# A three-block model on one core: convolution taps beside the in-projection, modulation rows beside the second down projection, running sums for norms

## The chip, the core and the metric

The kernel runs on one core of a Trainium2 chip. The metric is device microseconds of one execution; three runs gave 4223.4, 4220.96 and 4223.6 us, median 4223.4. All data is fp32; large products are made from a rounded part and a rest of each operand (three matmuls for one).

## The reference, cut to what matters

A sequence of 512 tokens of width 1024 goes through three blocks. What the change touches:

```
# first block
x = layer_norm(ALPHA*x + 0.5*swiglu(x, ffn1...), ln1)
q, f_raw, i_val, g_out, conv_val, conv_gate = split(x @ w_in)      # 6 x 512 columns
o_a = hgrn2(q, f_raw, i_val) ... * sigmoid(g_out)
u = conv_val * sigmoid(conv_gate)
c = depthwise_causal_conv(u, conv_w)  + conv_b                     # 31 taps, 512 channels
o_b = silu(layer_norm(c))
x = layer_norm(ALPHA*x + concat(o_a, o_b) @ w_out, ln2)
x = layer_norm(ALPHA*x + 0.5*swiglu(x, ffn2...), ln3)
# second block
mod = silu(c) @ w_ada + b_ada                                      # 1024 x 6144, one row of c
h = rms_norm(x) * (1 + scale1) + shift1 ; x = x + gate1 * (mixer(h) @ w_out)
h = rms_norm(x) * (1 + scale2) + shift2 ; x = x + gate2 * experts(h)
# third block
x = x + mixer3(rms_norm(x)) @ w_out ; x = x + relu(rms_norm(x) @ w_ff1)**2 @ w_ff2
out = rms_norm(x)
```

## The kernel before

Features lie on the 128 partitions, tokens along the free axis, so x is 8 feature blocks of 128 x 512.

`linear` (L274) is one projection. Weights come as units through a ring of four slots, fetched by SyncE: 8 feature blocks (512 KB) a unit, or 11 (704 KB) in the down projections of the first block, where an output block is two units (m = 2). VectorE splits each unit into a rounded part (L382) and a rest (L71), two units at a time being held; TensorE does 24 or 33 matmuls of 128 x 512 with it (L347); ScalarE (`act_out`) or VectorE (`dve_out`) evicts. VectorE's order in a body is: split the next block's units, wait for this block's matmuls, evict. Bodies are run in hardware loops. Stages given as `stages` run ahead of the first unit in the same block of code: VectorE splits the first two units, and then does its part of the stages.

`Norm` (L102) sums over features on TensorE with a matrix of ones: with centering first the mean (L152, 8 matmuls) and the subtraction (L194), then squares on ScalarE (L171), their sum (L158, 8 matmuls), root (L175), reciprocal on VectorE (L198), scaling (L205), bias (L180), and the split into parts (L184, L71). In the profile one fp32 matmul is two records, so 8 are "x16".

In the first block, `in_projection_and_modulation` (L497) runs the 24 units of the in-projection; beside each, SyncE fetches two rows of w_ada (128 x 1024, 512 KB each, ring of four) and VectorE multiplies and adds them (L530, L532). `hgrn_and_conv` (L607) then runs four blocks of code, each ending in a barrier:
- a first step: 48 one-column matmuls that end the modulation (L636), gates, logarithm, scan (L650), u (L654);
- transposes of v and k into rows (L717, copies L695, exponential L706);
- the score loop, 7 levels and a first one: VectorE makes distances (L760, L761), ScalarE the exponential (L807), GpSimd one product (L747) and VectorE the other (L794), TensorE the scores (L834), VectorE the masked copies (L766). Beside it run the convolution's taps: 62 on VectorE for feature blocks 2 and 3 (L776, L780), 62 on TensorE for 0 and 1 (L839), each with a diagonal matrix from ScalarE (L811), two in turn;
- the output step (L861 to L923).

After it comes the convolution's norm in a block of its own, then the out-projection, whose weights are fetched when it begins. The second feed-forward follows with its down projection (8 blocks of 66 matmuls, VectorE evicting at L433), then the second block, whose first stage is the third layer norm followed by an RMS norm.

What orders the work is the order written for each engine and semaphore waits between them:

```
for k in (2 * j, 2 * j + 1):                          # L526 and on, beside unit j of body i
    dve.wait_ge(ada_landed[k % 4], i * 32 + (k // 4 * 16 + 16))
    ...
    dve.wait_ge(multiplied, i * DB + (k + 1))
    dve.sem_inc(rows_used, 1)
```

Of the kernel before, what the change touches and what calls it, by code (L numbers as in the profile page):

```python
# [76 lines left out]

class Split:
# [17 lines left out]
    def vector(self, dve):  # L96
        for k in range(self.kb):
            dve.wait_ge(self.hi_ready, k + 1)
            self.parts.rest(self.p.nc, (slice(None), k, slice(None)), self.src[:, k, :]).then_inc(self.lo_ready, 1)


class Norm:  # L102
# [7 lines left out]
    def __init__(self, p, ctx, src, dst, kb, width, eps, gain, bias=None, center=True, func=ACT.Identity,  # L110
                 parts=None, first=0, after=None, squares=None, rstd=None, root_in_bank=False):
        self.p, self.src, self.kb, self.width, self.eps = p, src, kb, width, eps
        self.gain, self.bias, self.center, self.func = gain, bias, center, func
        self.parts, self.first, self.after = parts, first, after
        halves = 1 if width <= 512 else 2
# [8 lines left out]
        else:  # L124
            self.rstd = p.sb(ctx, "rstd", [P, width])[:] if rstd is None else rstd
        self.mean_ready, self.centered, self.sq_ready, self.sq_used, self.eps_set, self.rms_ready, self.rstd_ready, \
            self.scaled, self.done, self.hi_ready, self.lo_ready = p.sems(
                ctx, "mean_ready", "centered", "sq_ready", "sq_used", "eps_set", "rms_ready", "rstd_ready",
                "scaled", "done", "hi_ready", "lo_ready")
# [16 lines left out]
    def tensor(self, pe):  # L146
        nc, kb = self.p.nc, self.kb
        if self.center:
# [5 lines left out]
            last.then_inc(self.mean_ready, 1)  # L154
        for k in range(kb):
# [6 lines left out]
    def scalar(self, act):  # L162
        nc, kb, center = self.p.nc, self.kb, self.center
        for k in range(kb):
# [9 lines left out]
        act.wait_ge(self.sq_used, kb)  # L174
# [12 lines left out]
    def vector(self, dve):  # L187
# [3 lines left out]
        if self.center:  # L191
            dve.wait_ge(self.mean_ready, 1)
            for k in range(kb):
                nc.vector.scalar_tensor_tensor(out=self.halved(self.dst[:, k, :]), in0=self.total(0), scalar=-1.0 / (kb * P),  # L194
                                               in1=self.halved(self.src[:, k, :]), op0=ALU.mult, op1=ALU.add) \
                    .then_inc(self.centered, 1)
        dve.wait_ge(self.rms_ready, 1)
        nc.vector.reciprocal(self.rstd, self.rstd).then_inc(self.rstd_ready, 1)  # L198
        dve.wait_ge(self.rstd_ready, 1)
        x = self.dst if self.center else self.src  # L200
        for k in range(kb + lag):
            if k < kb:
                if self.dst is None and k >= self.slots:
                    dve.wait_ge(self.lo_ready, k - self.slots + 1)
# [6 lines left out]
        dve.wait_ge(self.scaled, kb)  # L211


class Placed:
# [16 lines left out]
    def vector(self, dve):  # L231
        pass

# [40 lines left out]
def linear(p, name, w, kb, nb, x, act_out=None, dve_out=None, width=T, x_from=0, slots=RING,  # L274
           sp_beside=None, before=None, stages=None, also=None):
# [14 lines left out]
    with ExitStack() as ctx:  # L290
# [28 lines left out]
        def _(sp):  # L319
# [8 lines left out]
            if bodies > 1:  # L328
                with sp.Fori(0, bodies - 1) as i:
                    body(i, False)  # L330
# [3 lines left out]
        def _(pe):  # L334
# [23 lines left out]
            if bodies > 1 or not front:  # L358
                with pe.Fori(1 if front else 0, bodies) as i:
                    body(i, False)  # L360

        @block.scalar
        def _(act):
# [4 lines left out]
            if act_out is not None:  # L368
                with act.Fori(0, bodies) as i:
                    for j in range(lot):  # L370
                        act.wait_ge(units_done, i * units + (j * m + m + 2))
                        ins = act_out(act, i, j, i * lot + j, psum(j), bank_free)
                        if ins is not None:
                            ins.then_inc(bank_free[j], 1)

        @block.vector
        def _(dve):
# [23 lines left out]
            split_block(0, 0)  # L401
            if front:
                if m == 1:
                    split_block(0, 1)
                for stage in front:
                    stage.vector(dve)
                if bodies > 1:
                    body(0, False, True)
            done = 1 if front and bodies > 1 else 0
            if bodies - 1 > done:  # L410
                with dve.Fori(done, bodies - 1) as i:
                    body(i, False)
            body(bodies - 1, True, bool(front) and bodies == 1)

# [14 lines left out]
def residual_out(p, x, gate):  # L429

    def out(dve, i, j, n, psum, bank_free):
        g = gate if isinstance(gate, float) else gate[:, bass.ds(n, 1)]
        return p.nc.vector.scalar_tensor_tensor(out=at_block(x, n), in0=psum, scalar=g, in1=at_block(x, n),  # L433
                                                op0=ALU.mult, op1=ALU.add)
# [62 lines left out]
def in_projection_and_modulation(p, x_parts, proj, c_cols, acc, stages, also):  # L497
# [5 lines left out]
    with ExitStack() as ctx:  # L503
        silu_c = p.sb(ctx, "silu_c", [P, DB])
        multiplied, rows_used = p.sems(ctx, "multiplied", "rows_used")
        with ExitStack() as c:
            silu_ready, = p.sems(c, "silu_ready")
            block = c.enter_context(nc.Block())

            @block.scalar  # L510
            def _(act):
                act.sem_inc(rows_used, 4)
                nc.scalar.activation(silu_c[:], c_cols[:, 0:DB], ACT.Silu).then_inc(silu_ready, 1)
                act.wait_ge(silu_ready, 1)

        with ExitStack() as c:
            ring = p.sb(c, "ada_ring", [P, 4, D])
            ada_landed = p.sems(c, *[f"ada_landed{u}" for u in range(4)])

            def sp_beside(sp, i, j):  # L520
                for k in (2 * j, 2 * j + 1):
                    sp.wait_ge(rows_used, i * DB + (k + 1))
                    sp.dma_start(ring[:, k % 4, :], d["w_ada"][k, :, bass.ds(i * D, D)]).then_inc(ada_landed[k % 4], 16)

            def dve_out(dve, i, j, n, psum, bank_free):
                at = at_block(acc, i)  # L526
                for k in (2 * j, 2 * j + 1):
                    dve.wait_ge(ada_landed[k % 4], i * 32 + (k // 4 * 16 + 16))
                    if k == 0:
                        ins = nc.vector.tensor_scalar(at, ring[:, 0, :], silu_c[:, 0:1], None, ALU.mult)  # L530
                    else:
                        ins = nc.vector.scalar_tensor_tensor(out=at, in0=ring[:, k % 4, :], scalar=silu_c[:, k:k + 1],  # L532
# [2809 lines left out]
```

## Time and profile before

| | |
|---|---|
| median of the runs | 4223.4 us |
| the profiled execution | 4229.67 us, span 4227.9 us |
| TensorE busy | 3774.1 us |
| VectorE busy | 2514.1 us |
| ScalarE busy | 1208.5 us |
| GpSimd busy | 341.5 us |
| mean granted TensorE clock | 0.941 |

Busy time is the time in which an engine runs an instruction; the granted clock is a share of full speed. In a row of a timeline the columns are start, length, engine, line, operation, output<-inputs and count, and in brackets how long the engine was idle before and what ended that.

### The profile page before, as it was taken

The numbers are of one execution on the slowest core, as the hardware profiler recorded it, in microseconds if no ns is written. First come the engines' busy times: TensorE is split into PE (matmuls) and PEld (weight loads), VectorE is DVE, ScalarE is ACT, GpSimd is POOL, SyncE is SP. The second block draws the span as 40 slices with busy tenths as digits, with TensorE's granted clock in tenths as the row PEclk, the third lists the DMA queues.
The fourth block names the chain that finished last, engine by engine and source line by source line (L and its number), as shares of the span: only waits on it lengthen the run. The fifth ranks groups of instructions, "written<-read, shape, count | busy, mean of one in ns | idle before, by whom it ended". The sixth has DMA issues, their size and how long they took to land. (4 is left out here: it accounts for less than half of the span.)

```text
span 4227.9 us, 51433 instructions
## 1 busy us (share of the span) xinstructions
PE 3774.1 (89%) x19109; PEld 3249.5 (77%) x19109; DVE 2514.1 (59%) x4080; ACT 1208.5 (29%) x2104; POOL 341.5 (8%) x276
## 2 busy tenths in 40 slices
PE   8998988799977987989999989999988889689998
PEld 7876764588756786689999979999857858566776
DVE  4544777554344463468999867777644437654433
ACT  1101132211021242233578843333321123403300
POOL 0000010000000020002212222222100000000000
PEclk9999988899988888999999999999989989789999
DMA  4222710222211001248889889999622111022232
GB/s 150 95 74 98 256 53 0 102 90 94 75 51 70 20 1 42 87 126 280 289 298 334 318 317 321 320 333 331 239 80 80 67 37 45 1 80 80 79 110 70
DMA packets 198961, 590.89 MB, mean 140 GB/s; under 512 B 22128, under 2 KB 80368, under 8 KB 196720
## 3 DMA queue, kind: packets, MB, share of 16 engines
q1 hardware_dynamic: 161920, 454.34, 31.5%
q0 software_dynamic: 36864, 134.23, 9.0%
q8 instruction: 106, 1.74, 0.2%
q14 instruction: 71, 0.58, 0.0%
HBM read 536.07 MB, written 52.43 MB: 139 GB/s over the span
## 5 line engine op out<-in xcount | busy, mean ns | idle before, releaser
L382 DVE CAST w_hi<-w_ring 128x1024 fp32r<-128x1024 f32 (+1 forms) x336 | 238.5, 710 | 585.9 <-PE banks L347 497.0
L71 DVE TENSOR_TENSOR w_lo<-w_ring,w_hi 128x1024 fp32r<-128x1024 f32 (+1 forms) x336 | 424.6, 1264 | 11.5
L2443 PE MATMUL out_ps<-w_hi,v_hi 128*128 128x384 f32 x1024 | 346.3, 338 | 45.2 <-DVE w_lo L71 45.2
L347 PE MATMUL banks<-x_hi,w_hi 128*128 128x512 f32 x896 | 356.5, 398 | 29.6 <-DVE x_lo L71 28.5
L2143 PE MATMUL up_ps<-h_hi,u_hi 128*128 128x384 f32 x1024 | 351.3, 343 | 19.7 <-DVE u_lo L71 19.6
L347 PE MATMUL banks<-x_lo,w_hi 128*128 128x512 f32 x896 | 354.4, 396 | 0.0
L347 PE MATMUL banks<-x_hi,w_lo 128*128 128x512 f32 x896 | 354.2, 395 | 0.0
L2443 PE MATMUL out_ps<-w_hi,v_lo 128*128 128x384 f32 x1024 | 344.7, 337 | 0.0
L2443 PE MATMUL out_ps<-w_lo,v_hi 128*128 128x384 f32 x1024 | 344.6, 337 | 0.0
L2143 PE MATMUL up_ps<-h_lo,u_hi 128*128 128x384 f32 x1024 | 343.9, 336 | 0.0
L2143 PE MATMUL up_ps<-h_hi,u_lo 128*128 128x384 f32 x1024 | 343.6, 336 | 0.0
L347 PE MATMUL banks<-h_hi,w_hi 128*128 128x512 f32 x576 | 235.1, 408 | 42.4 <-DVE h_lo L71 23.5
L347 PE MATMUL banks<-hidden_hi,w_hi 128*128 128x512 f32 x608 | 239.6, 394 | 21.8 <-DVE w_lo L71 21.8
L347 PE MATMUL banks<-hidden_lo,w_hi 128*128 128x512 f32 x608 | 239.1, 393 | 0.0
L347 PE MATMUL banks<-hidden_hi,w_lo 128*128 128x512 f32 x608 | 238.5, 392 | 0.0
L2443 PEld LDWEIGHTS out_ps<-w_hi,v_hi 128*128 128x128 f32 x1024 | 194.4, 190 | 50.4 <-DVE v_lo L71 50.4
L347 PE MATMUL banks<-h_lo,w_hi 128*128 128x512 f32 x576 | 231.5, 402 | 0.0
L347 PE MATMUL banks<-h_hi,w_lo 128*128 128x512 f32 x576 | 231.3, 401 | 0.0
L2457 ACT ACTIVATE v_hi<-expert_tiles 128x1024 fp32r<-128x1024 f32 x128 | 135.7, 1060 | 332.7 <-PE out_ps L2443 249.6
L347 PEld LDWEIGHTS banks<-x_hi,w_hi 128*128 128x128 f32 x896 | 169.6, 189 | 76.2 <-issue 21.2
L347 PE MATMUL banks<-hn_hi,w_hi 128*128 128x264 f32 (+1 forms) x704 | 186.6, 325 | 39.5 <-DVE w_lo L71 31.6
L2143 PEld LDWEIGHTS up_ps<-h_hi,u_hi 128*128 128x128 f32 x1024 | 193.8, 189 | 23.1 <-DVE u_lo L71 22.6
(537 smaller groups left out, 7773.8 us busy)
## 6 DMA issues: line engine op xcount, KB each, us to landing
expert_tiles<-peer_u SPq DMA_DIRECT2D x128, 512.0 KB
expert_tiles<-peer_v SPq DMA_DIRECT2D x128, 512.0 KB
w_ring<-w_in SPq DMA_DIRECT2D x104, 512.0 KB, 4.4
w_ring<-ffn_up SPq DMA_DIRECT2D x88, 512.0 KB, 3.5
w_ring<-w_ff SPq DMA_DIRECT2D x64, 512.0 KB, 3.8
ada_ring<-w_ada SPq DMA_DIRECT2D x48, 512.0 KB, 5.6
peer_acts<-act_ring SPq DMA_DIRECT2D x128, 192.0 KB
peer_gates<-staging SPq DMA_DIRECT2D x12, 2048.0 KB
```

Of the source, the lines that this page charges most:

```text
L71: return nc.vector.tensor_tensor(self.lo[at], value, self.hi[at].bitcast(F32), ALU.subtract)
L347: last = nc.tensor.matmul(banks[:, j, s, 0:n], a[:, u % 2, k, :], b[:, g * kg + k, x_from + c:x_from + c + n], start=(g == 0 and k == 0 an ...
L382: nc.vector.tensor_copy(w_parts.hi[:, u % 2], ring[:, u % slots]).then_inc(hi_ready, 1)
L2143: last = nc.tensor.matmul(up_ps[:, n % 3, 0:DENSE], a[:, n % 2, k, :], b[:, k, P:T], start=(k == 0 and part_ == 0), stop=(k == DB - 1 and ...
L2443: last = nc.tensor.matmul(out_ps[:, b, P:T], a[:, n % 2, b * P:b * P + P], r[:, n % 2, :], start=(n == 0 and part == 0), stop=(n == NKEYS ...
L2457: nc.scalar.activation(v.hi[:, n % 2, :], slot(n), ACT.Copy).then_inc(v_hi_ready, 1)
```

## The change

- The in-projection's units are in another order: convolution value and gate, f, g, q, v. Evictions apply the sigmoid where one is wanted. After unit 8, VectorE multiplies value and gate into a padded buffer, and in 15 turns after it does the 62 taps of its two blocks. Bodies are written out rather than looped.
- The taps of the other two blocks stay on TensorE, 14 in the first step, 17 in the transposes (between the four of v and the four of k) and 31 in the score loop, three or four a level.
- The 48 modulation rows go beside the second down projection, six in each of its 8 blocks, three fetched by SyncE per unit; TensorE's one-column matmuls follow bodies 1, 2 and 3. The silu of c is taken at the start.
- `Tally`: VectorE keeps a running sum of x (or of its squares) as a projection updates x. The norm behind it then needs one matmul for the mean, or for the squares where it doesn't center. It is used in the three layer norms of x, before the query projection, before ff1 and in the last norm.
- In a norm with centering, weights are split after centering; in one whose squares come from a tally, the first unit is split after the reciprocal and the second at the end.
- The convolution's norm becomes a stage of the out-projection. The weights of out2 are fetched before the second block's mixer.

```diff
+class Tally:
+    def take(self, dve, x, n):
+        dve.wait_ge(self.updated, n + 1)
+        dve.wait_ge(self.added, n + 1)
+        if self.squares:
+            nc.vector.tensor_tensor(self.scratch, at_block(x, n), at_block(x, n), ALU.mult).then_inc(self.squared, 1)
+            dve.wait_ge(self.squared, n + 1)
+            nc.vector.tensor_tensor(self.total, self.total, self.scratch, ALU.add).then_inc(self.added, 1)
+        else:
+            nc.vector.tensor_tensor(self.total, self.total, at_block(x, n), ALU.add).then_inc(self.added, 1)
...
 class Norm:
     def tensor(self, pe):
-        if self.center:
+        if self.center and self.tally is not None:
+            nc.tensor.matmul(self.total(0), self.p.ones, self.tally.total, start=True, stop=True).then_inc(self.mean_ready, 1)
+        elif self.center:
...
+        if self.sums_of == 1:
+            nc.tensor.matmul(self.total(0), self.p.ones, self.tally.total, start=True, stop=True).then_inc(self.sq_used, 1)
+            return
...
+    # in the in-projection, VectorE after unit (i, j):
+            if (i, j) == (2, 0):
+                for c in range(4):
+                    nc.vector.tensor_tensor(upad[:, c, TAPS - 1:], proj[:, c, :], proj[:, 4 + c, :], ALU.mult).then_inc(u_ready, 1)
...
+            for n in range(len(own_taps) * at // len(turns), len(own_taps) * (at + 1) // len(turns)):
...
+class Modulation:
+    def sync(self, sp, i, u):
+        first = (4 * i + u) * 3
+        for r in range(first, first + 3):
+            if r + ADA_RING < ADA_ROWS:
+                sp.wait_ge(self.multiplied, r + 1)
+                self.fetch(sp, r + ADA_RING)
+    def vector(self, dve, i, j):
+        first = (2 * i + j) * 6
+        for r in range(first, first + 6):
+            dve.wait_ge(self.landed[r % ADA_RING], 16 * (r // ADA_RING + 1))
...
+                dve.wait_ge(self.multiplied, r)
+                ins = nc.vector.scalar_tensor_tensor(out=at, in0=row, scalar=c, in1=at, op0=ALU.mult, op1=ALU.add)
+    def tensor(self, pe, i):
+        for g in ((), (0, 1), (2,), (3, 4, 5))[i]:
+            pe.wait_ge(self.multiplied, DB * g + DB)
+            for k in range(DB):
+                last = self.p.nc.tensor.matmul(self.sums[:, g * DB + k:g * DB + k + 1], self.acc[:, g, k * P:k * P + P],
+                                               self.p.ones[:, 0:1], start=True, stop=True)
...
     # hgrn_and_conv, transposes
             @block.scalar
             def _(act):
+                diagonals(act, 14, 18)
                 act.wait_ge(rel, 1)
                 nc.scalar.activation(decay[:, 0, :], decay[:, 0, :], ACT.Exp).then_inc(rel_exp, 1)
+                diagonals(act, 18, TAPS)
...
                 for g in range(8):
+                    if g == 4:
+                        convolve(pe, 14, TAPS)
...
     # score loop
-                    convolve(l)
...
+                    diagonals(act, *group(l))
...
+                    convolve(pe, *group(s))
...
+            def split_mix(c2):
+                first = Split(p, c2, mix, mix_parts, 4)
+                return [first, Norm(p, c2, mix[:, 4:8, :], mix[:, 4:8, :], 4, T, BETA_LN_EPS, cg, bias=cbeta, func=ACT.Silu,
+                                    parts=Section(mix_parts, 4, 8), lo_ready=first.lo_ready, lo_from=4)]
```

## Rows read from the trace of the kernel before

**Rows 1.** The page, busy time of each engine, share and instructions.

```profile
PE 3774.1 (89%) x19109; PEld 3249.5 (77%) x19109; DVE 2514.1 (59%) x4080; ACT 1208.5 (29%) x2104; POOL 341.5 (8%) x276
```

**Rows 2.** Stages: us, each engine busy (xinstructions), PEclk, DMA share, GB/s.

```profile
414.50:557.80 143.30, 138.67 (x576) 108.49 (x576) 107.78 (x103) 21.86 (x37) 0.00 (x0) 0.98 0.66 227
557.80:578.50 20.70, 19.76 (x96) 19.70 (x96) 10.03 (x9) 10.17 (x8) 0.00 (x0) 0.53 0.00 1
578.50:590.70 12.20, 7.03 (x32) 6.12 (x32) 9.45 (x10) 3.19 (x2) 1.80 (x1) 0.67 0.00 1
590.70:700.00 109.30, 90.44 (x381) 58.49 (x381) 101.20 (x115) 37.38 (x72) 22.75 (x9) 0.92 0.00 1
...
1084.00:1209.80 125.80, 122.25 (x528) 100.67 (x528) 45.12 (x40) 0.00 (x0) 0.00 (x0) 0.97 0.21 69
```

**Rows 3.** Timeline of the in-projection, ScalarE's evictions and VectorE's modulation rows.

```profile
424.05 0.60 ACT L425 ACTIVATE proj<-banks 128x512 f32 x1 [1.88 <-PE banks L347]
...
452.25 1.28 DVE L532 SCALAR_TENSOR_TENSOR acc<-ada_ring,silu_c,acc 128x1024 f32 x1 [1.32 <-DMA ada_ring<-w_ada]
...
453.68 1.29 DVE L532 SCALAR_TENSOR_TENSOR acc<-ada_ring,silu_c,acc 128x1024 f32 x1 [0.15 <-DVE acc L532]
...
555.13 0.60 ACT L425 ACTIVATE proj<-banks 128x512 f32 x1 [4.99 <-PE banks L347]
```

**Rows 4.** Timeline of the score loop, VectorE, TensorE and GpSimd.

```profile
622.55 3.73 PE L834 MATMUL score_ps<-kd 128*128 128x128 f32 x32
...
639.53 5.38 DVE L780 SCALAR_TENSOR_TENSOR mix<-upad,conv_w,mix 128x512 f32<-128x512 f32 x8
...
644.83 2.55 DVE L766 COPY_PREDICATED scores<-masks,score_ps 128x512 f32<-128x512 int32 x4
...
648.59 1.23 DVE L760 TENSOR_TENSOR decay<-b 128x1024 f32<-128x1024 f32 x1
...
653.34 7.04 PE L839 MATMUL conv_ps<-upad,diag 128*128 128x512 f32 x16
...
660.97 3.19 POOL L747 TENSOR_TENSOR kd<-proj,decay 128x1024 f32<-128x1024 f32 x1 [7.80 <-ACT decay L807]
...
662.05 3.19 DVE L760 TENSOR_TENSOR decay<-b 128x1024 f32<-128x1024 f32 x1
```

**Rows 5.** Timeline of the first step of the recurrence, TensorE.

```profile
558.20 19.76 PE L636 MATMUL sums<-consts,acc 128*128 128x1 f32 x96 [3.20 <-PEq L290]
```

**Rows 6.** Timeline of norms and of the out-projections' starts, TensorE and VectorE.

```profile
389.75 7.11 PE L152 MATMUL sums<-x,consts 128*128 128x512 f32 x16 [2.63 <-PEq L506]
...
752.01 0.69 DVE L382 CAST w_hi<-w_ring 128x1024 fp32r<-128x1024 f32 x1 [4.73 <-DMA w_ring<-w_out]
...
764.17 0.69 DVE L433 SCALAR_TENSOR_TENSOR x<-banks,x 128x512 f32<-128x512 f32 x1 [3.53 <-PE banks L347]
...
804.82 8.80 PE L152 MATMUL sums<-x,consts 128*128 128x512 f32 x16 [2.61 <-PEq L42]
...
1211.99 10.04 PE L152 MATMUL sums<-x,consts 128*128 128x512 f32 x16 [3.00 <-PEq L1164]
...
1636.67 0.69 DVE L382 CAST w_hi<-w_ring 128x1024 fp32r<-128x1024 f32 x1 [4.18 <-DMA w_ring<-w_out]
...
1690.09 9.94 PE L158 MATMUL sums<-squares,consts 128*128 128x512 f32 x16 [3.51 <-ACT squares L171]
```

**Rows 7.** Second down projection on VectorE; landings of w_ada's rows, 440 to 500; a window of 5 us.

```profile
1119.27 0.89 DVE L382 CAST w_hi<-w_ring 128x1408 fp32r<-128x1408 f32 x1 [4.93 <-PE banks L347]
...
1121.74 0.68 DVE L433 SCALAR_TENSOR_TENSOR x<-banks,x 128x512 f32 x1
...
1136.70 0.68 DVE L433 SCALAR_TENSOR_TENSOR x<-banks,x 128x512 f32 x1
...
DMA to landing us min/median/max: 4.2/6.2/7.2
...
809.00:814.00 5.00, 4.62 (x11) 1.71 (x9) 3.42 (x6) 0.00 (x0) 0.00 (x0) 1.00 1.02 419
```

More of the change, by code:

```diff
@@ L114, in __init__ @@
         self.parts, self.first, self.after = parts, first, after
+        self.tally, self.lo_from = tally, lo_from
+        self.sums_of = 1 if tally is not None and not center else kb
         halves = 1 if width <= 512 else 2
@@ L163, in scalar @@
         nc, kb, center = self.p.nc, self.kb, self.center
-        for k in range(kb):
+        for k in range(kb if self.sums_of == kb else 0):
             if center:
@@ L211, in vector @@
         dve.wait_ge(self.scaled, kb)
+        if first_weights is not None and self.sums_of == 1:
+            second_weights()
 class Placed:
@@ L326, in body @@
                         sp_beside(sp, i, u)
-            if bodies > 1:
+            if unrolled:
+                for i in range(bodies - 1):
+                    body(i, False)
+            elif bodies > 1:
                 with sp.Fori(0, bodies - 1) as i:
@@ L357, in _ @@
                 body(0, True)
-            if bodies > 1 or not front:
+            if unrolled:
+                for i in range(1 if front else 0, bodies):
+                    body(i, False)
+                    if tensor_beside is not None:
+                        tensor_beside(pe, i)
+            elif bodies > 1 or not front:
                 with pe.Fori(1 if front else 0, bodies) as i:
@@ L367, in _, with evict @@
                 stage.scalar(act)
-            if act_out is not None:
-                with act.Fori(0, bodies) as i:
[L370 to L374, printed above, removed]
+            def evict(i):
+                for j in range(lot):
+                    act.wait_ge(units_done, i * units + (j * m + m + 2))
+                    ins = act_out(act, i, j, i * lot + j, psum(j), bank_free)
+                    if ins is not None:
+                        ins.then_inc(bank_free[j], 1)
+            if act_out is not None and unrolled:
+                for i in range(bodies):
+                    evict(i)
+            elif act_out is not None:
+                with act.Fori(0, bodies) as i:
+                    evict(i)
         @block.vector
@@ L409, in _ @@
             done = 1 if front and bodies > 1 else 0
-            if bodies - 1 > done:
+            if unrolled:
+                for i in range(done, bodies - 1):
+                    body(i, False)
+            elif bodies - 1 > done:
                 with dve.Fori(done, bodies - 1) as i:
@@ L494, with in_projection_and_convolution @@
 GROUP = 8
-def in_projection_and_modulation(p, x_parts, proj, c_cols, acc, stages, also):
+def in_projection_and_convolution(p, x_parts, proj, upad, conv_w, conv_b, mix, tables_landed, stages, also):
     nc, d = p.nc, p.dram
     with ExitStack() as ctx:
[L504 to L532, printed above, removed]
-                                                             in1=at, op0=ALU.mult, op1=ALU.add)
-                    ins.then_inc(multiplied, 1)
-                    dve.wait_ge(multiplied, i * DB + (k + 1))
-                    dve.sem_inc(rows_used, 1)
-            linear(p, "in1", d["w_in1"], DB, 24, x_parts, act_out=copy_out(p, proj), dve_out=dve_out,
-                   sp_beside=sp_beside, stages=stages, also=also)
@@ L634, in _ @@
             def _(pe):
-                for n in range(6 * DB):
-                    last = nc.tensor.matmul(sums[:, n:n + 1], acc[:, n // DB, n % DB * P:n % DB * P + P],
-                                            p.ones[:, 0:1], start=True, stop=True)
-                last.then_inc(summed, 1)
+                convolve(pe, 0, 14)
             @block.vector
@@ L3211, in _first_arrays @@
     lb = a["lb_logits"]
+    w_in1 = tiled(a["w_in"][0])
     return {
```

336 lines of the change are left out of this document (218 added, 118 removed).

## The prediction

> **What bounds the kernel now.** I read the page first. TensorE is busy 89% of the span and VectorE 59% [rows 1], so the dense stretches are TensorE's, and a change can only win where TensorE idles, runs at the low clock, or does little work per microsecond. The table by stage shows where that is [rows 2]. The in-projection takes 143.3 us for 24 units. The first step after it takes 20.7 us at a granted clock of 0.53, the transposes 12.2 us, the score loop 109.3 us (VectorE busy 101.2, TensorE 90.4) and the second down projection 125.8 us with VectorE busy only 45.1. The three places that the change works on are thus a loop bound by VectorE (score loop), a stage with idle VectorE (second down), and norm prologues in which everything waits in a chain.
>
> The profiled execution took 4229.7 us against a median of 4223.4, so 6.3 us more (0.15%); I work out a difference and subtract it from the median. About 0.2% (8.4 us) is what a measurement of this kernel can tell from no change.
>
> **In-projection.** Evictions of unit 1 and unit 24 begin at 424.05 and 555.13 [rows 3]: 131.1 us for 23 units, 5.70 each. A down block, 66 matmuls, takes TensorE 14.96 [rows 7], so 24 would take 5.44. The excess comes from the modulation rows: VectorE waits 1.32 us for a row's DMA, then needs 1.43 us per row [rows 3]. With rows gone, 62 taps of 0.67 us (8 in 5.38, [rows 4]) are spread over 15 turns: at most 5 x 0.67 + 1.9 for the weight split = 5.2, under 5.44. TensorE covers them, with 0.2 us to spare in the fullest turn. So 23 x 0.26 = -6.0; the last turn's 5 taps (3.4) instead of two rows (2.7) give +0.8. **-5.**
>
> **First step and transposes.** The first step was set by 96 one-column matmuls with their weight loads, 19.8 us [rows 5]. Now TensorE does 14 taps there, at 0.88 us (16 halves in 7.04, [rows 4]) 12.3 us, but ScalarE makes the diagonals in order with the logarithm: four, then the log, then ten. Log done at about 8 us, ten taps after it 8.8, end 17.5 to 19 (the first two taps at the half clock). **-2.** In the transposes TensorE gets 17 taps, 15.0 us, between transposes that took 12.2 in all [rows 2]. ScalarE's exponential queues behind four diagonals, of which two wait for taps, so it starts near 6 instead of 2.4; then 13 taps (11.4), four transposes and the last copy: about 22.5. Nothing covers these taps. **+11** (+9 to +14).
>
> **Score loop.** It loses 62 VectorE taps, 41.6 us, and half of TensorE's 62 [rows 4]. Per level VectorE keeps two distances 2.4, four masked copies 2.5 and one product 1.2 = 6.1; the chain product, score matmuls 3.73, last copy 0.7, product 1.2 is 6.0 too. TensorE keeps 3.73 + 4 taps 3.5 = 7.2 [rows 4], so TensorE sets the pace, 7.3 with a semaphore. Filling: first distance, exponential, GpSimd product, masked copies, about 9 us to the second level's scores; 6 x 7.3; then 3.7 + 3.5 + the eviction 0.7. That is 61 to 62 against 109.3. GpSimd is the unknown: a distance that takes 1.22 alone took 3.19, ending 1.1 us after GpSimd's product did [rows 4]. If the distance, the copies and the product are all held up by it, a level costs 6.1 + 2.8 = 8.9 and the stage 72. I take the former and 1 us of loss, since the product falls beside the copies, which read PSUM. **-46** (-36 to -49).
>
> The Trainium skill, SBUF — State Buffer, "Who interferes with whom", says that a VectorE instruction with two SBUF inputs is fully blocked while a GpSimd instruction that reads SBUF runs, and that one with at most one SBUF input is not. The trace agrees for the distances; no row has a masked copy beside GpSimd's product. By that rule a level stays at 7.3.
>
> **Convolution norm and out-projection.** The norm becomes a front stage: weights are fetched before it, their splits run while squares are summed, and the first four blocks' splits run beside the mean. Now the splits begin only at 752.0, after 4.7 us of waiting for weights that are fetched once the norm is done [rows 6]; its reciprocal ended at 744.5. After: reciprocal ends 744.8, scaled blocks 2.7, then 1.27 per block; unit 1 ends near 753 where it ended at 764.1 (first eviction 764.17, [rows 6]). **-11** (-9 to -12).
>
> **Layer norms with a running sum.** For the three means TensorE's 16 halves of 7.11, 8.80 and 10.04 us [rows 6] become two, 0.9 at the full or 1.7 at the half clock. The last add lies on the path: 0.69 + 0.15 wait. What comes next is late too: the squares now start after little TensorE work, and a start at the low clock costs some 1.7, as the second mean beside the first shows. First: -7.1 + 0.9 + 0.85, a silu block removed (-0.9), perhaps part of the 1.7: **-5**. Second: -8.8 + 1.7 + 0.85 + 1.9: **-4.5**. Third: -10.0 + 1.7 + 0.85 + 1.9: **-5.5**. Weight splits fit behind the centering (4.9 + 3.8 < squares and root).
>
> **Norms without mean.** Squares and their sums go (9.94 us in the query norm, [rows 6]; over 7 in the others) with 1 to 3 us ahead of them; a multiply and an add on VectorE (1.7) and one TensorE sum (1.7) come. But the splits now stand behind the reciprocal: 1.9 on the path, and 1.9 at the end, of which 1 shows. Query norm **-4**, third feed-forward **-2**, final norm (no weights) **-4.5**. Out2's weights come before the mixer, so a wait like out1's 4.7 [rows 6] goes, less what the splits (3.8) now show: **-3**. Start: one silu and perhaps its table load: **+0.5** (0 to 1.6). The GpSimd clears, and the other down projections' adds (1.7 in turns with over 4 idle), I cost at nothing: VectorE's idle time hides them; uncovered, 0.8 a block.
>
> **Second down projection.** A block of 66 matmuls takes 14.96 us, VectorE's weight splits 2 x 2.47 of it [rows 7]. Added per block: 0.84 for the sum and six rows. Five rows at 1.43 and one at 0.90 make 8.1, so a block's VectorE chain from "block done" to "next weights split" is 2.47 + 0.68 + 0.84 + 8.1 + 2.47 + 0.3 of semaphores = 14.8. That is 0.2 under TensorE; the two blocks without a short row run 0.4 over. The ring holds four rows, six are wanted in a burst: row 5 is issued 1.4 us into it and wanted at 5.7, so a landing over 4.3 stalls. Landings were 4.2 at least, 6.2 median, in a loaded stage, 7.2 at most [rows 7]. I take 5: 0.7 a block, **+5** (0 to 24). On TensorE come 96 halves of one column. They took 0.206 each at the granted half clock [rows 5], half of it is the bound below. Two groups after body 1, one after body 2: 9.9 us (5 to 10), in which VectorE catches up, and they may bring the half clock into the dense matmuls behind them, 2 us each time: **+9**. The tail: after the last block VectorE still has six rows (8.6), then TensorE's last group 3.3, then the addition: **+13**. Together **+27** (+18 to +46). SP passes each weight fetch behind a row's wait; the latest is issued 6 us before its split, near the median landing.
>
> The Trainium skill, DMA: Bandwidth & Descriptors, "Specifications", gives some 358 GB/s from HBM per core. Down's 36.7 MB in 120 us are 306 GB/s, and bursts go above 358. The trace shows 419 GB/s in a stretch of 5 us [rows 7], so I don't let bandwidth bind; by the page's figure the bursts would queue, which is rival 2.
>
> **Sum.** 0.5 - 5 - 5 - 2 + 11 - 46 - 11 - 4.5 + 27 - 5.5 - 3 - 4 - 2 - 4.5 = -54. 4223.4 - 54 = **4169**.
>
> **Rivals.** (1) GpSimd holds up every VectorE step of a level: 8.9 a level, +11: 4180. For it: distances of 3.19 us. Against: the copies read PSUM. 0.18. (2) Rows land as late as the worst seen, 7.2: rows 5 and 6 stall 3 us a block, +24 instead of +5: 4188. 0.14. (3) More gain: score loop at 7.2 with warm transposes, one-column matmuls at the full clock, no row stalls: some 18 better, 4151. 0.13. (4) **Slower:** in the second down projection the row ring starves. It decides from a landing of about 12 us, where the stall is 7.5 a block and eats the gain; at 14 us, 9.8 x 8 = 78 in place of 5: 4242. Nothing seen landed so late. 0.03. (5) The taps aren't hidden in the in-projection: turns over 5.44 give back 0.5 x 15 = 8 and more elsewhere, up to no change at 4223: 0.04. The forecast has 0.48.
>
> The range takes the bounds of score loop, down projection and clocks: 4148 to 4196. Chances: faster 0.93, same 0.03, slower 0.04.
>
> **What would show it.** Right: evictions 5.44 apart in the in-projection; score loop near 62 us with TensorE over 90% busy; transposes near 22; second down near 151 with a 13 us tail; a first matmul of the third norm 5 us earlier. Wrong: levels of 9 us with distances over 3 us; row waits over 1 us in every block; taps pushing splits late in the in-projection.

## The result, and the profile after

Four runs gave 4166.99, 4193.64, 4167.66 and 4174.52 us, median **4171.1**, against 4223.5 for the kernel before beside them; the ratio is 0.9884, 95% interval 0.9846 to 0.9922: faster clear of the noise, by less than 2%. The forecast was 4169, range 4148 to 4196, so time and direction held. The profiled executions stand further apart: 4229.7 before, 4167.0 after, -62.7; the one was 6 us over its median, the other 4 below. The stages below are measured in these two.

The line of busy times on the page, after:

```profile
PE 3723.9 (89%) x19025; PEld 3216.6 (77%) x19025; DVE 2556.6 (61%) x4155; ACT 1189.2 (29%) x2077; POOL 345.6 (8%) x281
```

TensorE is as busy by share as before [rows 1], on 50 us less work. The 84 records fewer are sums of norms: six norms, 14 each. The work from the first step to the end of the score loop, with the one-column sums wherever they stand, takes 13 us less, at a higher clock.

The table by stage, after: in-projection, first step, transposes, score loop, second down projection. Columns as in [rows 2].

```profile
409.70:551.90 142.20, 137.81 (x576) 109.63 (x576) 92.58 (x121) 23.17 (x37) 0.00 (x0) 0.98 0.22 67
551.90:569.70 17.80, 15.60 (x28) 6.21 (x29) 7.62 (x7) 8.68 (x19) 0.02 (x1) 0.81 0.00 0
569.70:592.30 22.60, 18.56 (x67) 9.77 (x67) 9.48 (x11) 9.69 (x19) 1.79 (x1) 1.00 0.00 1
592.30:657.10 64.80, 57.30 (x318) 39.75 (x319) 55.69 (x53) 24.90 (x41) 19.20 (x7) 1.00 0.00 1
...
1026.90:1174.40 147.50, 136.02 (x624) 113.63 (x624) 105.34 (x98) 0.00 (x0) 0.14 (x1) 0.94 0.64 227
```

Against [rows 2] the score loop is 44.5 us shorter and TensorE's clock in it is 1.00 instead of 0.92; the transposes are 10.4 longer because TensorE has taps to do there (x67 instead of x32); the second down projection carries 96 more matmul records and 105 us of VectorE.

One level of the loop, VectorE, then GpSimd; last, the first level's masked copies and the product beside them (timeline after):

```profile
609.55 3.19 DVE L974 TENSOR_TENSOR decay<-b 128x1024 f32<-128x1024 f32 x1
612.67 1.21 DVE L975 TENSOR_TENSOR decay<-b 128x1024 f32<-128x1024 f32 x1
613.80 2.55 DVE L980 COPY_PREDICATED scores<-masks,score_ps 128x512 f32<-128x512 int32 x4
616.24 1.22 DVE L992 TENSOR_TENSOR kd<-proj,decay 128x1024 f32<-128x1024 f32 x1
617.57 3.22 DVE L974 TENSOR_TENSOR decay<-b 128x1024 f32<-128x1024 f32 x1
...
608.68 2.98 POOL L961 TENSOR_TENSOR kd<-proj,decay 128x1024 f32<-128x1024 f32 x1 [3.91 <-ACT decay L1002]
617.37 2.34 POOL L961 TENSOR_TENSOR kd<-proj,decay 128x1024 f32<-128x1024 f32 x1 [5.70 <-ACT decay L1002]
...
596.83 2.63 DVE L980 COPY_PREDICATED scores<-masks,score_ps 128x512 f32<-128x512 int32 x4
...
596.68 2.98 POOL L961 TENSOR_TENSOR kd<-proj,decay 128x1024 f32<-128x1024 f32 x1 [25.19 <-ACT decay L1002]
```

A level takes 8.02 us (609.55 to 617.57; the next two 8.03 and 8.05, the figure used below), and VectorE has no idle time over 0.2 us in it. The first distance takes 3.2 instead of 1.2: it runs while GpSimd's product does and ends 1.1 us after it. TensorE would need about 7.2 (scores 3.73 and four taps of 0.86).

The second down projection, by its new rows (view of the tile of modulation rows; the last figure of a line is the count):

```profile
its engine sat idle before it (us, times) until:
  DMA ada_ring<-w_ada: 12.5, 11
who waited for it (us, times):
...
  PE mod_sums L724: 6.8, 1
```

VectorE waits 12.5 us for rows, yet TensorE idles for only one late weight split (2.3 us at 1076.0). It waits 6.8 us ahead of the last group of one-column sums, for the last six rows: that is the tail.

TensorE at and behind the first two groups of one-column sums (us, PE busy and matmuls started, clock, DMA share, GB/s):

```profile
1090.90:1094.80 3.90, 3.90 (x35) 1.00 1.03 418
1094.80:1098.20 3.40, 3.40 (x9) 0.50 0.38 102
1098.20:1101.60 3.40, 3.40 (x16) 1.00 0.87 269
```

In the 3.4 us behind the groups the granted clock was 0.50, the lower of its two levels, and 9 large matmuls started where 15 or 16 do at 1.00: 1.7 us lost. Behind the single group at 1126.3 the clock stayed at 1.00.

### The profile page after: what moved, and what is told of

Its sections match the earlier page's. It is cut to its first block and busy times, and to the rows that moved or that the text cites. A ratio compares the mean times of both kernels' runs of the same rounds, so it can differ in the third digit from the quotient of the medians.

```text
span 4165.2 us, 50974 instructions
## 1 busy us (share of the span) xinstructions
PE 3723.9 (89%) x19025; PEld 3216.6 (77%) x19025; DVE 2556.6 (61%) x4155; ACT 1189.2 (29%) x2077; POOL 345.6 (8%) x281
## 5 line engine op out<-in xcount | busy, mean ns | idle before, releaser
L2331 PE MATMUL up_ps<-h_hi,u_hi 128*128 128x384 f32 x1024 | 351.3, 343 | 20.0 <-DVE u_lo L71 19.9
L438 PE MATMUL banks<-hidden_hi,w_hi 128*128 128x512 f32 x608 | 240.5, 396 | 22.4 <-DVE w_lo L71 22.4
```

The lines of the kernel that those rows point to most:

```text
L438: last = nc.tensor.matmul(banks[:, j, s, 0:n], a[:, u % 2, k, :], b[:, g * kg + k, x_from + c:x_from + c + n], start=(g == 0 and k == 0 an ...
L2331: last = nc.tensor.matmul(up_ps[:, n % 3, 0:DENSE], a[:, n % 2, k, :], b[:, k, P:T], start=(k == 0 and part_ == 0), stop=(k == DB - 1 and ...
```

## The experiments

**1. Operand places.** The trace of after held something that no step of the prediction explains: the out-projection's units lay 5.60 us apart where they were 5.44 before, with the same matmuls at the full clock. Counting starts, the large matmuls of nearly every stage follow one another at 226.7 ns or at 233.3 ns (two in the third block lie between them, at 231.7 and 232.6). The edit moves each norm's 4-byte epsilon column out of the stage's memory:

```
-        self.eps_col = p.sb(ctx, "eps_col", [P, 1])
+        p.norms = getattr(p, "norms", 0) + 1
+        self.eps_col = p.eps_cols[:, p.norms % 8:p.norms % 8 + 1]   # one tile, allocated at the start
```

> In both traces a stage's large matmuls follow one another at 226.7 ns or at 233.3 ns, the same through a whole stage, and the out-projection went from the one to the other with this change (units 5.44 apart before, 5.60 after). In the built program the weight parts of the stages at 226.7 start a multiple of 512 bytes from the activation parts; where it is 233.3, each norm's epsilon column has shifted them by 32 (64 before the second block's first projection). Here the columns lie in one tile ahead of everything, so that all differences are 0. Theory A (places of the two operands): all stages go at 226.7: 3168 matmuls x 6.67 ns = 21 us less, about 4150; units of the in-projection and out-projection 5.44 apart. Rival B (the norm ahead of the stage, which leaves TensorE or its bank order in another state): no change, 4171, all paces as they were. Rival C: paces change but VectorE's turns with five taps (3.40 + 1.9) then bind in the in-projection: 17 to 20 us less.

Measured: 4161.6 us median of four (4150.2 to 4164.8); ratio to before 0.9842 (0.9812 to 0.9871). The intervals of the two ratios overlap, so the runs alone don't settle the size; the traces do. (The kernel before, run beside the experiments, gave medians of 4228 to 4232 us; times from different experiments can be compared only that closely.) TensorE in windows inside dense stretches (us, PE busy and matmuls started in them, clock, DMA share, GB/s): first up projection, in-projection, out-projection, second up. After:

```profile
40.00:240.00 200.00, 200.00 (x884) 1.00 0.31 94
430.00:530.00 100.00, 100.00 (x430) 1.00 0.27 85
710.00:740.00 30.00, 30.00 (x130) 1.00 0.11 36
800.00:1000.00 200.00, 200.00 (x859) 1.00 0.30 92
```

With the epsilon columns moved (in-projection, out-projection, second up):

```profile
430.00:530.00 100.00, 100.00 (x442) 1.00 0.28 85
710.00:740.00 30.00, 30.00 (x134) 1.00 0.12 36
800.00:1000.00 200.00, 200.00 (x884) 1.00 0.29 92
```

"PE busy 200.00 at clock 1.00" is the same in both, and yet 884 matmuls start in place of 859. From first to last matmul the in-projection took 134.3 us instead of 137.8, the second up projection 242.9 instead of 249.8, the third feed-forward's 179.6 instead of 184.4; these, the out-projection, the second block's first projection and the queries, six stages, together 20.8 less. The span fell by 16.8; some 3 us came back between the in-projection and the out-projection, in the output step and norm, whose code is unchanged, where TensorE's granted clock was lower in this execution (0.79 instead of 0.87). Rival C is out: the in-projection's evictions lie 5.44 apart, with the turns of five taps inside.

The stage between the two rates that is easiest to work out fits as well. The gates projection of the third block goes at 231.7 ns in the mean, in after and with the columns moved alike. Its activations have rows of 528 tokens, so from one feature block to the next the difference of the two addresses changes by 64 bytes modulo 256 and is 0 in one block of four: (226.7 + 3 x 233.3) / 4 = 231.7.

**2. The same from the other side**, by padding ahead of the weight parts, norms untouched:

```
+        pad = {'up1': 32, 'down1': 64, 'in11': 96, 'out11': 480, 'up2': 64, 'gm1': 448,
+               'peer_q1': 224, 'out21': 96, 'ff21': 64}.get(stage, 0)
+        if pad: p.sb(ctx, "pad", [P, pad // 4])
         w_parts = Parts(p, ctx, "w", [P, 2, kg, P])
```

> The other half of the test: padding alone, norms as they are. Difference between weight and activation parts, modulo 512 bytes: first up projection 32, first down projection 64, in-projection 128, out-projection 0, second up projection 96, second down 0, second block's first projection 0, its out-projection 128, queries 256, third feed-forward up 32 (as now), down 64. Theory A: the stages at 0 go at 226.7 ns with their norms still ahead of them; the first up and down projections, which have no norm ahead, rise to 233.3 (7 and 3.5 us more); 128 and 256 tell whether the modulus is 128, 256 or 512. Rival B: first up, first down and last down stay at 226.7, those with a norm ahead stay at 233.3.

Its windows: first up (difference 32), first down (64), in-projection (128), out-projection (0), second up (96), the second block's out-projection (96), queries (256), third up (32), third down (64). The expectation has 128 for the second block's out-projection, but it stood at 0 in after and its pad is 96 bytes (`out21`), so it is 96.

```profile
40.00:240.00 200.00, 200.00 (x858) 1.00 0.30 92
290.00:380.00 90.00, 90.00 (x387) 1.00 0.23 72
430.00:550.00 120.00, 119.76 (x514) 1.00 0.26 79
730.00:760.00 30.00, 30.00 (x134) 1.00 0.12 36
800.00:1000.00 200.00, 200.00 (x856) 1.00 0.29 92
1615.00:1650.00 35.00, 35.00 (x151) 1.00 0.10 31
1680.00:1740.00 60.00, 58.79 (x259) 1.00 0.30 96
3800.00:3940.00 140.00, 138.68 (x593) 1.00 0.30 91
4000.00:4150.00 150.00, 150.00 (x645) 1.00 0.29 89
```

The first up projection fell from 884 to 858 starts and took 248.3 us instead of 241.4, the first down 124.5 instead of 121.0; the out-projection rose to 134 with its norm still ahead of it, and so did the second block's first projection (difference 0). The windows of the queries and of the third up projection have gaps between units; from start to start their matmuls went at 226.8 and 233.3 ns. So 0 and 256 give 226.7 to 227 ns; 32, 64 and 128 give 233.1 to 233.3; 96 gives 234.3 in both stages that have it. Theory A stands, with a modulus of 256 bytes, and rival B falls. It is the difference that counts and not the place of one operand: in the built programs the first up projection has both operands at 0 modulo 256 in before, at 32 in after and at 64 in experiment 1, and goes at 226.7 ns in all three. Why the chip does this is not shown. The run took 4191.5 us once, with five stages slower than in after and three faster.

**3. Who holds up the distance.** GpSimd's operation (L961) goes onto VectorE, ahead of its own product (L992); the GpSimd part is removed.

```
+                    nc.vector.tensor_tensor(half_runs(kd[:, l % 2, :], l, 0), half_runs(k, l, 0),
+                                            half_runs(decay[:, l % 2, :], l, 0), ALU.mult).then_inc(k_ready, 1)
                     nc.vector.tensor_tensor(half_runs(kd[:, l % 2, :], l, 1), half_runs(q, l, 1), ...
```

> The score loop's products of the first halves move from GpSimd to VectorE. Theory L (the 0.8 us that a level is longer than predicted, 8.05 instead of 7.3, come from the one distance that GpSimd's product holds up for 2.0 us, 3.2 instead of 1.2): a level has 2 x 1.21 + 2.55 + 2 x 1.2 = 7.4 on VectorE, loop 60 to 62 us instead of 64.8. Rival (the distance is slow for another reason, such as waiting for ScalarE or the writes of the masked copies): 8.05 + 1.2 = 9.25 a level, loop near 73.

One level:

```profile
610.70 1.22 DVE L965 TENSOR_TENSOR decay<-b 128x1024 f32<-128x1024 f32 x1
611.85 1.22 DVE L966 TENSOR_TENSOR decay<-b 128x1024 f32<-128x1024 f32 x1
612.98 2.54 DVE L971 COPY_PREDICATED scores<-masks,score_ps 128x512 f32<-128x512 int32 x4
615.42 1.20 DVE L983 TENSOR_TENSOR kd<-proj,decay 128x1024 f32<-128x1024 f32 x1
616.55 1.22 DVE L985 TENSOR_TENSOR kd<-proj,decay 128x1024 f32<-128x1024 f32 x1
617.86 1.23 DVE L965 TENSOR_TENSOR decay<-b 128x1024 f32<-128x1024 f32 x1
```

A level is 7.16 us with one operation more on VectorE, the loop 60.7 instead of 64.8. GpSimd's help cost more than it gave. This is the rule of the Trainium skill, SBUF — State Buffer, "Who interferes with whom", that I weighed: the distances have two SBUF inputs and are blocked. That the masked copies, with the scores in PSUM and only the mask in SBUF, aren't is now shown too: in after, four of them took 2.63 us from 596.83, wholly beside a product of 2.98 from 596.68, where undisturbed ones take 2.55. The run's time, 4175.9 once, says nothing on 4 us.

**4. The modulation left out.** No fetches, rows or one-column sums; the modulation is then the bias alone, so the later blocks compute other values.

```
-        for r in range(first, first + 6):
+        for r in range(0):
-        for g in ((), (0, 1), (2,), (3, 4, 5))[i]:
+        for g in ():
```

> Leaves out the modulation rows: no fetch, no multiply and add, no one-column sums (the modulation is then the bias alone). What the second down projection costs more than before is then only the running sum. Theory by terms: 145.4 - 11 (one-column sums, 96 halves of 0.113) - 8 to 9 (tail: last six rows, sum, addition) - 2.3 (TensorE waiting for a split behind late rows) = 123 to 124, the total about 22 us less. Rival: part of the 22 us is SP's weight fetches being late behind the rows' waits or the clock; then blocks without rows are still over 15.1 apart and the stage stays near 128.

From the last matmul of the second up projection to the first of the next block took 172.9 us (1029.7 to 1202.6) instead of 195.6 (1021.2 to 1216.8): **22.7** are the modulation. The run took 4152.9 us once. The stage itself went in 121.6 from first to last matmul, no more than before the change, so the running sum costs TensorE nothing there. The terms inside the stage are a double and a single bare group of sums (3.6 and 1.8), 1.7 at the low clock behind the first and 2.3 of TensorE idle; behind it comes a tail of the running sum and six rows (9.5), the last group (3.6, at clock 0.50) and the addition. The other 3.6 us, a double group, runs beside the last rows. So VectorE's 12.5 us of waiting for rows cost TensorE those 2.3 us inside the stage.

**5. TensorE's taps back in the loop**, none in the first step and the transposes:

```
-                return TAPS + TAPS * s // (LEVELS + 1), TAPS + TAPS * (s + 1) // (LEVELS + 1)
+                return 2 * TAPS * s // (LEVELS + 1), 2 * TAPS * (s + 1) // (LEVELS + 1)
```

> All 62 of TensorE's taps go back into the score loop, none in the first step and the transposes. By the terms of the prediction: the first step falls from 17.9 to the chain of logarithm and scan, about 12; the transposes from 22.6 to the 11.9 that they had before (TensorE's taps there are bare); the score loop has 3.73 + 7.75 taps of 0.88 = 10.6 a level, 8 of them and the filling: 88 to 92 instead of 64.8. Sum: +7 to +11. Rival: the taps in the first two blocks were bare and the score loop had room for them (VectorE bound at 8.05 with TensorE at 7.2), so the loop grows by less than 22 and the sum is below 0.

First step, transposes and loop:

```profile
553.50:564.00 10.50, 0.00 (x0) 0.01 (x1) 7.58 (x7) 3.50 (x5) 0.01 (x1) 0.50 0.00 0
564.00:576.20 12.20, 7.29 (x32) 6.55 (x33) 9.54 (x10) 3.18 (x2) 1.80 (x1) 0.50 0.00 0
576.20:660.90 84.70, 83.50 (x380) 53.26 (x381) 47.48 (x53) 37.34 (x71) 17.72 (x7) 0.98 0.00 1
```

107.4 us against 105.2 after. The first two match (-7.3 and -10.4), the loop grew by 19.9, below the 23 to 27 expected. TensorE is busy for 83.5 of its 84.7 us, which is eight levels of about 10.6 and none of the filling that the expectation had added. **Moving 31 taps out of the loop was worth 2.2 us**, as these three stages show it in one execution of each kernel; both theories missed the sum, the rival by less. (The run's time, 4184.5 once, was 13 over the median of after; most of that arose in stages which this edit doesn't touch.)

**6. VectorE's taps back in the loop**, the largest part undone alone (L654 runs there, 8 a level, and not beside the in-projection):

```
                     if l + 1 < LEVELS:
                         distance(l + 1)
+                    own(l)
                     take(l)
```

> Undoes the largest part alone: the 62 taps of VectorE go back from the in-projection into the score loop, 8 a level; TensorE's taps stay where the change put them. By the terms: the in-projection is no shorter, since it runs at 24 units of 24 matmuls of 233.3 ns (5.60 each) either way, but its tail of 3.4 us of taps goes (-3.4); the score loop grows by 62 x 0.67 = 41.6 to about 106, VectorE busy over 95%, the product of GpSimd now covered by taps or not by a microsecond or two a level. Sum about +38, 4209. Rival 1 (the taps are not free in the in-projection: they push weight splits late): units come closer together there and the sum is +30 or less. Rival 2 (the gain in the loop came from taking TensorE's taps out, not VectorE's): the loop stays under 85.

The loop's window:

```profile
592.00:694.00 102.00, 67.39 (x318) 49.84 (x319) 98.44 (x115) 24.91 (x41) 19.14 (x7) 0.83 0.00 1
```

The loop is 102.0, VectorE 98.4 of it; the in-projection to the first step is 139.2 instead of 142.2. So +37.2 and -3.0, +34 by stages; the whole took 4207.9 once, 37 over the median of after. Theory by terms holds, both rivals fall: the taps of VectorE make the change, and beside the in-projection they cost their tail of 3 us alone. TensorE, 67 us busy in 102, had a granted clock of 0.83 here instead of 1.00.

**7. No running sums.**

```
-                take = residual_out(p, x, 0.5 / ALPHA, tally)
+                take = residual_out(p, x, 0.5 / ALPHA)
-            return [Norm(p, c, x, x, DB, T, BETA_LN_EPS / ALPHA ** 2, g, b, parts=parts, tally=tally, **room)]
+            return [Norm(p, c, x, x, DB, T, BETA_LN_EPS / ALPHA ** 2, g, b, parts=parts, **room)]
```

and likewise for the other five.

> No running sums: all norms sum eight blocks again, squares on ScalarE; placement, front stages and splits stay. Theory by terms: +5 at the first layer norm (less 0.9 for the silu block that stays removed), +5 to 6 at the second and third each, +4 to 5 at the queries, +2 to 4 at the third feed-forward, +3.5 at the last norm, -0.8 for the add behind each last block is in these; together +22 to +28. Rival: the sums on TensorE had also kept it busy ahead of the first dense matmuls, which then start at the full clock; then it costs only 12 to 16.

4190.6 once, the span 23.6 over that of after. From the last matmul ahead of each norm to the first behind it: +3.9, +3.8, +3.0 (with the modulation's tail in between), +4.4, +4.1, and +4.2 at the end: 23.4, within the theory. Why it is less than the sums that went shows in the first norm. After, TensorE's sums are

```profile
389.71 1.10 PE L206 MATMUL sums<-tally,consts 128*128 128x512 f32 x2 [2.63 <-PEq L42]
392.25 8.52 PE L220 MATMUL sums<-proj,consts 128*128 128x512 f32 x16 [1.45 <-ACT proj L233]
```

and without the running sum

```profile
389.53 7.11 PE L211 MATMUL sums<-x,consts 128*128 128x512 f32 x16 [1.90 <-PEq L42]
398.08 7.13 PE L220 MATMUL sums<-proj,consts 128*128 128x512 f32 x16 [1.45 <-ACT proj L233]
```

Six us of mean go, and the squares behind them take 1.4 longer: the granted clock was 0.83 beside them in after, with 1.1 us of TensorE work just ahead, and 1.00 here, with 7.1. The rival had this effect at another place (the dense matmuls) and its size wrong.

**8. Four diagonals and a ring of seven rows**, in stages 450 us apart:

```
-        diag = p.sb(ctx, "diag", [P, 2, P])
+        diag = p.sb(ctx, "diag", [P, 4, P])
-ADA_RING = 4
+ADA_RING = 7
```

> Two parts in different stages. (a) Four diagonal buffers instead of two: in the first step and the transposes TensorE waits 2 to 2.3 us for diagonals that stand behind ScalarE's logarithm and exponential (1.28 of table load and 1.91 of work each). Theory: both waits go, first step 17.9 to 16, transposes 22.6 to 20.5. Rival: the exponential then stands behind more diagonals and the transposed keys come later: no gain. (b) A ring of seven modulation rows instead of four in the second down projection: theory: the row waits, 12.5 us in 11, fall under 3, but only the 2.3 us in which TensorE idled come back, and perhaps 1 to 2 of the tail: -3 to -4. Rival: the fetches are held by SP's order or the other transfers, not by the ring: waits stay.

First step, transposes, loop:

```profile
553.30:568.30 15.00, 13.74 (x28) 5.84 (x29) 7.69 (x8) 8.44 (x19) 0.11 (x1) 0.89 0.00 0
568.30:588.30 20.00, 18.28 (x66) 9.85 (x66) 9.40 (x10) 9.28 (x19) 1.71 (x1) 1.00 0.00 1
588.30:655.60 67.30, 58.94 (x318) 41.44 (x318) 57.12 (x53) 25.77 (x40) 18.36 (x7) 0.97 0.00 1
```

-2.8 and -2.6, a little over the 1.9 and 2.1 expected, but +2.5 in the loop:

```profile
596.93 3.73 DVE L974 TENSOR_TENSOR decay<-b 128x1024 f32<-128x1024 f32 x1
...
604.17 3.07 DVE L992 TENSOR_TENSOR kd<-proj,decay 128x1024 f32<-128x1024 f32 x1
```

In this one level GpSimd's products hold both a distance (3.73) and VectorE's own product (3.07 in place of 1.20), and it takes 10.4 us; in the levels behind it the own product is held in place of the distance. Every row wait is gone (12.5 us before), with landings of 3.9 to 8.4, median 6.3 (after: 3.6 to 8.7, median 5.7), and from the up projection to the next block it is 2.4 shorter: that is what 12.5 us of waits were worth. The run took 4172.5 us once. The Trainium skill, DMA: Bandwidth & Descriptors, "Specifications", gives some 358 GB/s per core. By that figure the bursts would queue; in after the stage moved 227 GB/s on the whole, and 418 in a stretch of 3.9 us, above that figure. What made VectorE wait was the ring of four: the same rows, landing no sooner, no longer keep it waiting.

**9. Together** (parts 1, 3 and 8):

> All parts that looked better, together: parts of both operands at equal places, the loop's product on VectorE, four diagonal buffers, ring of seven rows. Sum of the parts if they add: -17 to -21, -4.5, -4, -3 = -28 to -32, about 4140 where the changed kernel has 4171. Rival: in the score loop TensorE at 3.73 + 4 taps of 0.86 = 7.17 and VectorE at 7.2 bind together, and in the in-projection the turns with five taps bind, so that less comes: 4150.

4140.5 us median of four (4131.9 to 4148.5), ratio to before 0.9797 (0.9767 to 0.9826). First step 14.9, transposes 20.0, loop 62.2. The forecast by adding the parts was 4140, so they add, as far as medians can tell.

**10. Rows ahead of the eviction**, on top of 9:

```
                     w_parts.rest(nc, (slice(None), u % 2), ring[:, u % slots]).then_inc(w_ready, 1)
+                    if rows is not None:
+                        rows(u - j * m)          # three modulation rows
...
-        for g in ((), (0, 1), (2,), (3, 4, 5))[i]:
+        for g in ((), (0, 1), (2, 3), (4, 5))[i]:
```

> As the combined kernel, and in the second down projection a block's six modulation rows stand in threes behind the two weight splits ahead of its eviction, where VectorE waits for TensorE anyway, instead of all six behind the eviction; the one-column sums are two groups after each of the last three bodies. Theory (of the 22.7 us that the modulation costs, some 9 are the last six rows behind the last block, bare): the stage gets 8 to 9 shorter, no TensorE idle of 6.2 us before the last group; the rest (10.9 of one-column sums) stays: 4131 where the combined kernel has 4140. Rival: the evictions now come behind the rows and the next splits behind them, so TensorE waits for weights in the middle of the stage: as much lost as gained.

The last block, VectorE, then TensorE's last group:

```profile
1135.23 8.22 DVE L722 SCALAR_TENSOR_TENSOR ada_sums<-ada_ring,silu_c,ada_sums 128x1024 f32<-128x1024 f32 x6
1143.37 0.68 DVE L553 SCALAR_TENSOR_TENSOR x<-banks,x 128x512 f32<-128x512 f32 x1
...
1142.87 4.18 PE L730 MATMUL mod_sums<-consts,ada_sums 128*128 128x1 f32 x32
```

The six rows now end as the block does, and nothing bare is left but the sums, which now follow TensorE's work at once and take 4.18 us for two groups, where one took 3.6 at clock 0.50. From up projection to the next block 187.7 us instead of 194.6, so 6.9 of the 8 to 9 expected. Median **4135.8** of five (4129.5 to 4140.9), ratio 0.9773 (0.9752 to 0.9795): the lowest median here, 2.3% under before, where the change gave 1.2%. The interval overlaps that of experiment 9, so that this is the faster of the two rests on the stage and not on the runs.

## Why the prediction was right, step by step

Predicted and measured, us, in the order of the sum; measured between the two profiled executions, from the first instruction of a stage to the first of the next, so that a figure can differ by some tenths from the windows above:

| step | predicted | measured |
|---|---|---|
| start | +0.5 | +0.4 |
| first layer norm | -5 | -4.8 |
| in-projection | -5 | -1.5 |
| first step | -2 | -2.8 |
| transposes | +11 | +10.7 |
| score loop | -46 | -44.5 |
| convolution norm and out-projection | -11 | -9.6 |
| second layer norm | -4.5 | -5.9 |
| second down projection | +27 | +22.4 |
| third layer norm | -5.5 | -6.2 |
| out2, queries, third feed-forward, last norm | -3 -4 -2 -4.5 | -3.6 -4.8 -4.6 -3.5 |

The output step (-1.4) and the experts (-2.5) moved without being predicted; their code is as before. Sum predicted -54, measured -62 to -63 in the two profiled executions, and -52 in medians. These executions lie further apart than the medians, and which stages hold that excess isn't known, so a term is measured to a microsecond or two at best. That the median came within 2 us of the forecast is partly luck: terms were off by up to 4.6 us, in both directions, and the four runs of after alone spread over 27 us. What held is the direction, the size of the large terms and, but for those below, their reason.

**Where a term was mis-sized.** *In-projection*: I set its floor at 24 x 5.44 from a down block [rows 7]. The down projection ran at 226.7 ns a matmul and the in-projection at 233.3, in both kernels, so its floor was 5.60, and removing the modulation could give 0.10 a unit and not 0.26 (23 x 0.10 less the 0.8 of the tail is the 1.5 measured). Evictions after are 5.60 apart; with the operands' places mended they are 5.44 (experiment 1), and the step comes out at the predicted size (138.7 us to the first step, 5.0 under before). That the taps are hidden was right (experiments 1 and 6). *Out-projection*: the chain of splits was right, but this stage fell from 226.7 to 233.3 ns, by a column of 4 bytes that its norm brought along: +1.3.

*Score loop*: "TensorE sets the pace, 7.3" was wrong; VectorE does, at 8.05, since one distance a level is held for 2.0 us. I had taken "1 us of loss" for the whole loop. The loop took 64.8 against the 61 to 62 of the forecast, and 60.7 once GpSimd's product was out of the way (experiment 3). "A level stays at 7.3" stood on GpSimd's product falling beside the copies. It fell beside a distance, and that a distance is held there, [rows 4] had shown. Rival 1, 8.9 a level, is out: the copies are not held.

*Second down*: row stalls were priced at 0.7 a block on TensorE; there were 12.5 us of stalls, and they cost 2.4 (experiment 8); the weight parts of two units are held ahead. Waits of over 1 us came in four of eight blocks, not in every one. The groups of sums were put at 9: they took 5.4 at the full clock, and the low clock behind them came once, 1.7 us, and not twice. Landings reached 8.7 us, later than the 7.2 of rival 2, without its 24 us. *Tail*: 13 predicted, 13.9 found from the last large matmul to the addition.

*Norms*: right in size to 1.4 us (the third feed-forward's to 2.6) and for the right reason, the slower start of the squares included (experiment 7).

Of the signs named, two failed: evictions 5.44 apart (5.60), and TensorE over 90% busy in the loop (57.3 of 64.8, 88%).

**Where the gain came from**, as far as parts were undone: VectorE's taps beside the in-projection 34 by stages (37 by one run), running sums 20 to 24, TensorE's taps ahead of the loop 2, against 22.7 paid for the modulation's new place. Not undone by themselves: the convolution's norm as a front stage (-9.6 in the table), the early weights of out2 (-3.6), and what the modulation's old place had cost.

## What to carry to other kernels

Put a vector chain beside a stage only after asking what its last turn leaves bare, and put it ahead of the wait for TensorE, not behind the eviction: the same six rows cost 7 us less there. Waits of an engine that runs two units ahead are worth a fraction of their length (2.4 of 12.5 us here); measure them by removing them. And before taking one stage's matmul pace for another's, count the starts per window: a busy share of 100% at the full clock hides 3%.

## What the runs showed of the hardware that I had not expected

Large matmuls (128 x 512, rounded fp32) start 226.7 ns apart when the weight parts and the activation parts begin at SBUF addresses equal modulo 256 bytes, and 233.1 to 234.3 ns apart when they differ by 32, 64, 96 or 128, at granted clock 1.00 in both cases. The eleven stages that the expectation of experiment 2 names and six of experiment 1 follow this without an exception. Here it was worth 20.8 us of 4165.

A GpSimd product beside VectorE cost VectorE 2.0 us for its 2.3 of work, and which operation it hits depends on timing: a distance in after, VectorE's own product in experiments 6 (2.7 to 2.9 us) and 8 (2.9 to 3.1). Not tried: GpSimd's product timed to fall on the masked copies, which it does not hold.
